# Two blocks of a network on one core: ScalarE makes the high parts of seven weight units, GpSimd only their low parts

## The reference

```python
h = rms_norm(x, norm_mix)
proj = h @ w_in                       # queries, keys, values of three mixers
o_a = nsa_mixer(...)                  # 4 heads: compressed, selected, window keys
#   compressed: hid = gelu(raw @ cmp_w1); kv_c = hid @ cmp_w2
o_b = dilated_mixer(...)              # 3 groups x 2 heads
o_c = stick_breaking_mixer(...)       # 6 heads
x = x + concatenate([o_a, o_b, o_c]) @ w_out
h = rms_norm(x, norm_mlp)
x = x + square(relu(h @ w_up)) @ w_down
```

## Time and profile before

| | us |
|---|---|
| median of 3 runs | 1229.25 |
| lowest and highest run | 1220.51, 1233.41 |
| the profiled execution, its own time | 1218.77 |
| its span, first to last instruction | 1216.9 |
| mean granted TensorE clock over the span | 0.958 |

### The profile page before, as it was taken

The page is one execution under the profiler, slowest core; times in us unless marked ns, Lnnn a source line. Parts: engine busy times, 40 slices in busy tenths (PEclk is TensorE's granted clock), DMA queues, the critical chain, the costliest instruction groups (busy, mean ns, idle before and its releaser), DMA issues. The chain is left out here.

```text
span 1216.9 us, 15972 instructions
## 1 busy us (share of the span) xinstructions
PE 1160.7 (95%) x5827; PEld 981.4 (81%) x5827; DVE 672.6 (55%) x1149; ACT 440.0 (36%) x867; POOL 448.3 (37%) x366
## 2 busy tenths in 40 slices
PE   7999999999898989999888989998999999999998
PEld 5888888888788888898876787687888888888887
DVE  7768876484666545484466865554842251350441
ACT  6386686351354432131423743342320020110110
POOL 0000000026512224978242031100566676666762
PEclk9999999999988889999987998879999999999999
DMA  6232332333200002333121011101323223233221
GB/s 232 87 104 87 104 121 87 143 105 100 84 25 18 19 18 70 121 98 127 55 69 36 1 36 35 35 1 34 122 87 104 102 88 102 88 103 103 86 103 52
DMA packets 27279, 97.18 MB, mean 80 GB/s; under 512 B 3024, under 2 KB 3408, under 8 KB 27088
## 3 DMA queue, kind: packets, MB, share of 16 engines
q1 hardware_dynamic: 27216, 96.32, 23.5%
HBM read 94.21 MB, written 2.10 MB: 79 GB/s over the span
## 5 line engine op out<-in xcount | busy, mean ns | idle before, releaser
L449 POOL TENSOR_TENSOR hold<-hold 128x2 f32<-128x2 f32 x115 | 35.6, 309 | 679.3 <-DVE rx L1604 265.1
L452 POOL TENSOR_TENSOR wl<-raw,wh 128x1024 fp32r<-128x1024 f32 x115 | 277.7, 2414 | 9.6
L952 PE MATMUL bank<-xh,wh 128*128 128x512 f32 x312 | 128.4, 411 | 10.3 <-DVE xl L1614 8.5
L450 POOL TENSOR_SCALAR wh<-raw 128x1024 fp32r<-128x1024 f32 x115 | 126.0, 1096 | 0.2 <-issue 0.2
L954 PE MATMUL bank<-xh,wl 128*128 128x512 f32 x312 | 123.5, 396 | 0.0
L953 PE MATMUL bank<-xl,wh 128*128 128x512 f32 x312 | 123.3, 395 | 0.0
L1568 ACT ACTIVATE arena<-arena 128x512 f32<-128x512 f32 x32 | 20.2, 633 | 251.5 <-DVE arena L2042 251.5
L952 PE MATMUL bank<-yh,wh 128*128 128x512 f32 x264 | 103.9, 394 | 3.1 <-issue 2.0
L671 PE MATMUL bank<-arena 128*128 128x64 f32 (+1 forms) x612 | 97.0, 295 | 8.4 <-DVE arena L784 5.1
L731 ACT ACTIVATE arena<-arena,negm 128x256 f32<-128x256 f32 (+4 forms) x136 | 66.4, 490 | 105.3 <-DVE negm L842 104.4
L953 PE MATMUL bank<-yl,wh 128*128 128x512 f32 x264 | 103.0, 390 | 0.0
(11 more groups left out here) (237 smaller groups left out, 2468.6 us busy)
## 6 DMA issues: line engine op xcount, KB each, us to landing
raw<-weight_units SPq DMA_DIRECT2D x173, 512.0 KB, 3.5
x<-x_in SPq DMA_DIRECT2D x4, 512.0 KB, 6.8
out_fm<-x SPq DMA_DIRECT2D x8, 256.0 KB, 2.1
arena<-tables SPq DMA_DIRECT2D x1, 1024.0 KB, 5.5
par<-params SPq DMA_DIRECT2D x1, 166.0 KB, 2.1
arena<-swa_table SPq DMA_DIRECT2D x1, 128.0 KB, 5.7
ident<-identity SPq DMA_DIRECT2D x1, 64.0 KB, 8.7
```

Source lines behind the costliest of these rows:

```text
L449: pool.tensor_tensor(hold[:], hold[:], hold[:], ALU.add).then_inc(held, 1)
L450: pool.tensor_scalar(wh[:, j, :], raw[:, j, :], 1.0, 1.0, ALU.mult, ALU.mult).then_inc(high_done, 1)
L452: pool.tensor_tensor(wl[:, j, :], raw[:, j, :], wh[:, j, :], ALU.subtract).then_inc(split_done, 1)
L952: pe.matmul(out, lh, rh, start=start, stop=False)
```

## The change

ScalarE makes the high parts of seven units, 85 to 91 (ACT_HIGH = 7 from U_G2 on): the four of G2 and the first three of G4. Two of these copies stand in front of the gelu, five behind the table load and in front of the evacuations of G2. They are counted in a semaphore of their own, `act_high`. GpSimd's new function `low_of_act` waits for it, makes the tiny addition on `hold`, which now carries the count of `high_done`, and then the low part. GpSimd's ranges around the seven units are split in two; unit 92 and all later ones stay as they were. Nothing moves on the other engines.

```diff
+ACT_HIGH = 7
+        act_high = sem("act_high")
+            def low_of_act(u):
+
+                pool.wait_ge(act_high, u - U_G2 + 1)
+                pool.tensor_tensor(hold[:], hold[:], hold[:], ALU.add).then_inc(high_done, 1)
+                pool.wait_ge(high_done, u + 1)
+                pool.tensor_tensor(wl[:, u % RING, :], raw[:, u % RING, :], wh[:, u % RING, :], ALU.subtract)\
+                    .then_inc(split_done, 1)
...
-            split_units(U_BOUT + BEGUN + 2, U_OUT2 + BEGUN)
+            split_units(U_BOUT + BEGUN + 2, U_G2)
+            for u in range(U_G2, U_G2 + ACT_HIGH):
+                low_of_act(u)
+            split_units(U_G2 + ACT_HIGH, U_OUT2 + BEGUN)
...
+            def high_for_pool(u):
+
+                act.wait_ge(loaded[u % RING], 16 * (u // RING) + 16)
+                act.wait_ge(units_done, u - RING + 1)
+                act.activation(wh[:, u % RING, :], raw[:, u % RING, :], ACT.Copy).then_inc(act_high, 1)
+
...
+            high_for_pool(U_G2)
+            high_for_pool(U_G2 + 1)
             for c in range(2):
                 wait_done(act, ("hid", c))
                 act.activation(hidt[0:31, c, :], B[BANK[("hid", c)]][0:31, 0:P], ACT.Gelu_apprx_tanh).then_inc(evac_a, 1)
             act.preload_act_table_set("natural_log_exp_and_others")
+            for u in range(U_G2 + 2, U_G2 + ACT_HIGH):
+                high_for_pool(u)
             raw_heads("G2", 384, r2, ar(A_VD, TB, 384))
```

## The result

| | before | after |
|---|---|---|
| median of 22 runs each, us | 1228.11 | 1236.86 |
| lowest and highest run | 1201.57, 1251.58 | 1219.06, 1245.56 |
| the profiled execution, its own time | 1218.77 | 1239.28 |
| its span | 1216.9 | 1237.2 |
| mean granted clock over it | 0.958 | 0.941 |

The ratio of the two is 1.0159 with a 95% interval of 1.0108 to 1.0209. This ratio takes of each kernel only the runs near its own fastest; over all runs the medians lie 8.75 us (0.7%) apart. The forecast was 5.1 us faster, with a range up to 1232. Both numbers lie on the other side.

The account below looks back on a forecast made before the run. The prediction took TensorE, busy 95% of the span, to bound the kernel. Two shorter waits and the clock behind each, 1.05 + 0.8 + 1.96 + 1.3 = 5.1 us, took the median from 1229.25 to 1224.1 us, range 1214 to 1232.

Parts of the forecast that it names:

- The queues of GpSimd and ScalarE: Seven high parts off GpSimd give back at most 7.3 us of queue; ScalarE's idle time covers its seven copies.
- First wait: TensorE's idle time in front of G2, for unit 85, falls from 2.04 to 0.99 us: -1.05.
- Clock behind it: Less time lost to TensorE's lower clock: in G2, behind the first wait, -0.8 us; behind the second, -1.3.
- Second wait: TensorE's wait of 1.96 us for GpSimd's unit 92, behind G2, goes with 1.6 us to spare: -1.96.
- The sum of the head: The two waits and the clock behind each: 1.05 + 0.8 + 1.96 + 1.3 = 5.1 us gained.
- Does it pass on?: Behind 586 us nothing tied to a fixed time binds, so the later work shifts whole and keeps the 5.1 us.
- rival 2: The attention stage gets one more half-level stretch of 23.8 us: +6.8 us in all, 1236; chance 0.10.
- the prediction's own sign of being wrong: Behind 600 us: the forecast is wrong if the time at half level moves by more than 10 us.
- rivals 2 and 3: Attention's half-level time falls otherwise: one stretch more, 1236 us (chance 0.10), or the long stretch gone, -17, 1212 (0.07).
- Rival 4: At the head of attention the gain turns into waits for VectorE or ScalarE: only -1.5 us, 1227.7; chance 0.08.

Follow-up runs that it names:

- e5: The changed kernel with 12 more matmuls of 512 columns, results overwritten, in front of G2: median 1209.8 us.
- e8: The kernel before with 11 more matmuls of 512 columns in step 1 of the second attention loop: median 1216.1 us against 1223.55 without them.

## Why the prediction was wrong, point by point

- **The queues of GpSimd and ScalarE: right.** L461 ran 7 times, 2.40 us in the median; ScalarE's copies took 1.06; the gelu was not late; unit 92's hold came 0.25 us behind the end of G2, its split took 3.69 us (3.66 forecast), with 0.9 to spare where 1.6 were forecast, since I had counted from the end of the last matmul, and the next can start before it (4.9 us behind G2, not 5.3).
- **First wait: -1.05 forecast, -0.76 measured (2.04 to 1.28).** The low part beside VectorE took 2.83 instead of 2.66, and it began 0.1 later than counted.
- **Clock behind it: -0.8 forecast, -1.6 measured** (18.34 to 16.77). I had halved it for want of a nearer row.
- **Second wait: -1.96 forecast, -2.4 measured.** From the last matmul of G2 to the first of unit 92 it took 7.29 us (579.08 to 586.37) and now takes 4.87, for the reason just given.
- **Clock behind it: -1.3 forecast, -1.4 measured.** From there to VectorE's group 6 it took 9.01 us (586.37 to 595.38) and now takes 7.63.
- **The sum of the head: 5.1 forecast, 6.1 measured.** What the head gained is 6.1 us in five profiles of kernels that have the change and no filler up to there (6.09, 6.14, 6.11, 6.11, 6.14), against 5.1 in the sum.
- **"Does it pass on?" failed, and with it the forecast.** The step reads "Nothing that is tied to a fixed time binds, so the rest shifts whole". The clock is: in every profile its changes lie on an even grid that does not start with the kernel. The 285 us from 575 on lost 0.11 x 285 = 31 us to the lower level in the profile before and 0.23 x 285 = 66 after; that is rival 2, and as each us lost is two at half level, some 70 us more at half level, it is also the prediction's own sign of being wrong (more than 10 us). I had given it 0.10, for two reasons that don't hold. I took the longest stretch of the page, 23.8 us, as the measure of the worst, +11.9; it was 61.44. And I took the place as drawn anew in each run, so that rivals 2 and 3 would even out. A rule was part of this: the Trainium skill (TensorE: Matmul & The Clock Gate, What's actually happening) has the window run free of the kernel. The traces agree so far: at 200 us of work the same instruction lies at places up to 1.5 us apart from profile to profile. They do not bear out what I made of it, that the place in the middle of the kernel is chance: the places of 14 profiles lie within 0.7 us of one another at 520 us of work, and the 61.44 us stretch came in three profiles of three with that arrival. Rival 2's own time, 1236, is the measured median to a microsecond, and that is luck: it was worked out as one more stretch of 23.8 us on top of a gain of 5.1, where the runs show one stretch longer by 48 us, a gain of 6.1 in the head, and a loss that differs from run to run.
- Rival 4's -1.5 us does not follow from its own terms: 5.1 less 1.96 and 1.3 leaves 1.8. It changes nothing in the range.
- The spread of the runs (1220.51 to 1233.41) should have been a question, not only a width. When runs of one kernel on one core lie 1% apart, something else than its instructions differs; here span x clock of before spreads by 3.2 us (one standard deviation) and the time by 12.5.

What stays open: the change is worth 6.1 us by the head, of which some 3 are clock right behind the two waits, and 5.6 by the medians of e5 and e8, but only 2.0 and 0.4 in the two pairs with fillers in the loop, whose falls still lie in different places. And each kernel's runs were profiled once or twice; the place of the others is inferred from their clock alone.

## What to carry to other kernels

Multiply each run's span by its mean granted clock before comparing two kernels, and see how the product moves with the loss among the runs of one kernel (here 0.15 to 0.19 us per us lost). If the products at equal loss say one thing and the times another, the clock undoes the edit, and here a few fillers in the right place were worth more than the edit. Look for stretches at the lower level in which TensorE is busy, since removing waits elsewhere will not end them; put dense work behind the wait at which they begin. And an edit that only shifts a stage in time is not neutral where a stage hangs on the edge of the lower level: try it with some dead work of different length in front before giving a verdict.

## What the runs showed of the hardware

- The lower level can last while TensorE works: 61.44 us at 0.50 with TensorE busy 97% of it, to the same length in three profiles.
- The place against the clock's changes narrows on the way: 14 profiles lie within 1.5 us of one another at 200 us of work, and within 0.7 us behind a stage with falls of its own. That the falls do this is argued, no run here shows it by itself.
- 12 matmuls without use, 2.7 us, made the kernel 31 us faster; 8 more made it 30 us slower; 8 more 27 us faster.
- A bias row of 128x512 on VectorE (L807, L820 in after) took 2.48 us beside GpSimd's two-input subtraction in after and 2.45 in before, and 0.43 at 598.75 us of before, with GpSimd idle. The subtraction took 2.83 and 2.66 beside it instead of 2.40.
